# Expert rows scattered by index to (choice, token) order, and a combine that reads plain tiles, in a two-layer mixture-of-experts kernel

## The reference, cut to what matters

```python
expert = g_idx * EXP_PER_GROUP + e_idx          # [n, 2]: two choices for each token, of 32 experts
...
ys = (jax.nn.silu(xb @ w1[e]) * (xb @ w3[e])) @ w2[e]     # for each block of rows of one expert e
...
out[token] = sum over its two choices of gate * ys[row of that choice]
```

## Time and profile before

| | |
|---|---|
| runs | 3020.61, 3024.97, 3027.89 us; median 3024.97 |
| profiled execution | 3028.9 us; span of its trace 3027.1 us |
| PE busy | 88% of the span, mean granted clock 0.935 |
| DVE, ACT, POOL busy | 41%, 22%, 14% |
| DMA | 594.60 MB, mean 196 GB/s |
| experts of layer 0 | about 1606 to 2140 us, 42 blocks |
| experts of layer 1 | about 2534 to 2972 us, 51 blocks |

### The profile page before, as it was taken

One profiled execution on the slowest core, in us unless ns is written; L12 is line 12 of the kernel. 1 busy time (PEld: TensorE's weight loads), 2 busy tenths in 40 slices (PEclk: granted clock), 3 DMA queues, 4 the chain that ended last, 5 costly groups with the idle time before them and its releaser, 6 DMA issues. The chain is left out here.

```text
span 3027.1 us, 44944 instructions
## 1 busy us (share of the span) xinstructions
PE 2662.8 (88%) x17074; PEld 1742.1 (58%) x17075; DVE 1226.9 (41%) x2425; ACT 652.6 (22%) x1342; POOL 414.1 (14%) x465
## 2 busy tenths in 40 slices
PE   7999989999999998989968998889698984898755
PEld 5877766488884574557545554445444642454333
DVE  5752367248999922127162111111513623222114
ACT  3540178120000010117131000000321631010002
POOL 3432012014440000000001100000100001121101
PEclk9999999999999999989988999999899996999877
DMA  3231320137545632120028889999722025999994
GB/s 141 91 126 60 137 78 26 63 100 234 209 182 224 243 139 76 41 78 1 28 76 328 355 353 421 411 413 387 260 86 91 1 88 216 353 386 382 404 420 148
DMA packets 137319, 594.60 MB, mean 196 GB/s; under 512 B 20336, under 2 KB 40588, under 8 KB 90608
## 3 DMA queue, kind: packets, MB, share of 16 engines
q1 hardware_dynamic: 86704, 359.25, 31.5%
q10 hardware_dynamic: 41808, 212.75, 17.6%
q0 software_dynamic: 8688, 21.00, 1.9%
HBM read 574.06 MB, written 33.69 MB: 201 GB/s over the span
## 5 line engine op out<-in xcount | busy, mean ns | idle before, releaser
L1406 DVE SCALAR_TENSOR_TENSOR psum<-weight_ring,condition_rows 128x1024 f32<-128x1024 f32 x192 | 268.1, 1396 | 16.0 <-issue 0.9
L174 PE MATMUL psum<-modulated,weight_ring 128*128 128x384 f32 (+2 forms) x640 | 228.7, 518 | 0.0
L2826 DVE COPY expert_hidden_turned<-psum 128x128 f32<-128x128 f32 (+1 forms) x93 | 32.6, 351 | 462.6 <-PE psum L2684 462.6
L2673 PE MATMUL psum<-weight_ring,slot_rows_turned 128*32 128x256 f32 x2176 | 145.9, 414 | 77.2 <-DMA weight_ring<-in_w_dram 46.1
L2662 PE MATMUL psum<-weight_ring,slot_rows_turned 128*64 128x256 f32 x1792 | 205.6, 383 | 0.6 <-issue 0.6
L174 PEld LDWEIGHTS psum<-modulated,weight_ring 128*128 128x128 f32 x640 | 121.4, 190 | 105.5 <-issue 51.0
L2754 ACT ACTIVATE expert_silu<-psum 64x256 f32<-64x256 f32 (+1 forms) x91 | 34.6, 380 | 659.5 <-PE psum L2662 347.7
L2662 PEld LDWEIGHTS psum<-weight_ring,slot_rows_turned 128*64 128x64 f32 x1792 | 127.5, 138 | 76.3 <-issue 16.9
L2691 PE MATMUL psum<-weight_ring,expert_hidden_turned 128*32 128x256 f32 (+1 forms) x1536 | 165.8, 441 | 0.0
L174 PE MATMUL psum<-ffn_hidden,weight_ring 128*128 128x512 f32 (+1 forms) x440 | 154.5, 514 | 4.1 <-DVE ffn_hidden L1451 4.1
L2812 DVE TENSOR_TENSOR expert_hidden<-expert_silu,psum 64x256 f32<-64x256 f32 (+1 forms) x93 | 39.2, 422 | 276.7 <-ACT expert_silu L2754 248.7
(11 more groups left out here) (476 smaller groups left out, 4332.8 us busy)
## 6 DMA issues: line engine op xcount, KB each, us to landing
third_stream_weights<-in_w_dram ACTq DMA_DIRECT2D x93, 2048.0 KB, 14.6
weight_ring<-in_w_dram SPq DMA_DIRECT2D x84, 2048.0 KB, 17.5
weight_ring<-in_w_ada_dram SPq DMA_DIRECT2D x24, 2048.0 KB, 9.2
weight_ring<-in_w_ffn_dram SPq DMA_DIRECT2D x11, 2048.0 KB, 12.3
weight_ring<-in_w_rnn_dram SPq DMA_DIRECT2D x8, 1536.0 KB, 6.6
weight_ring<-in_w_att_dram SPq DMA_DIRECT2D x6, 2048.0 KB, 8.1
weight_ring<-in_w_in_dram SPq DMA_DIRECT2D x6, 2048.0 KB, 13.5
weight_ring<-in_w_down_dram SPq DMA_DIRECT2D x8, 1408.0 KB, 6.2
```

What stands on the lines that cost most here:

```text
L174: last = nc.tensor.matmul(out, weights[:, k * P:(k + 1) * P], rhs(k), start=(k == 0), stop=(k == tiles - 1))
L1406: last = v.scalar_tensor_tensor(out=product, in0=w[:, t], scalar=1.0, in1=CR[:, n, :], op0=ALU.mult, op1=ALU.mult, accum_out=c.mod[:, i // ...
L2673: last = nc.tensor.matmul(ps[units.rows(2 * m + o), 2 + b, 0:256], XT[:, b, k % tiles, units.rows(k // tiles)], w[:, k, 256 * o:256 * (o + ...
L2826: v.tensor_copy(HT[:, b, :, :], ps[:, 1, 0:256].rearrange("p (k s) -> p k s", k=2)[:, :, 0:2 * cap])\
```

## The change

Each expert block is no longer stored in place by ACT. POOL scatters it with an indirect DMA, 128 partial rows by index, to a DRAM tensor of 2 x 768 rows in (choice, token) order; rows of empty slots have an index past the end and are skipped. `route` computes a second index table for it, `R.home`, from which `R.index` is now derived with two more VectorE instructions, and no longer computes `R.slot`. The combine reads plain tiles of 128 rows, issued by SP. Since every row that is read has been written, the zero fill is gone. Three scatters whose indices are all past the end are issued before the loop, so that the counts of the semaphores begin at 16.

The core of the diff:

```diff
@@ feed_forward
-                written = UNITS[0].least * UNITS[0].cap
-                sp.dma_start(c.expert_out[written:, :], c.ios["zeros"].partition_broadcast(SLOTS - written))\
-                    .then_inc(zeros_in, 16)
                 ring.uses += len(order)
                 ring.feed(sp, ring.uses + Ring.SLOTS)
-                sp.wait_ge(zeros_in, 16)
@@ second_setup
-    c.expert_out = nc.dram_tensor("expert_rows", (SLOTS, D), F32, kind="Internal").ap()
+    c.expert_out = nc.dram_tensor("expert_rows", (2 * T, D), F32, kind="Internal").ap()
@@ route
-                v.scalar_tensor_tensor(out=R.slot[:, :, 0:nt], in0=blk, scalar=float(cap), in1=place,
-                                       op0=ALU.mult, op1=ALU.add)
...
-                v.tensor_scalar(R.index[:, 0:nblk], ps[:, 5, 0:nblk], const("half"), None, ALU.add).then_inc(placed.sem, 1)
+                to, wrapped, own = BL[:, 0, 0, 0:nblk], BL[:, 0, 1, 0:nblk], float(units_of.groups * units_of.tokens)
+                v.tensor_scalar(to, ps[:, 5, 0:nblk], const("half"), None, ALU.add)
+                dve.drain()
+                v.tensor_scalar(wrapped, to, own, -own, ALU.is_ge, ALU.mult)
+                dve.drain()
+                v.tensor_tensor(R.index[:, 0:nblk], to, wrapped, ALU.add).then_inc(placed.sem, 1)
+                v.tensor_copy(R.home[:, 0:nblk], to)
@@ experts, POOL
-                with pool.Fori(0, rounds(pool)) as it:
+                def store_at(b):
+                    pool.indirect_dma_start(out_rows, bass.IndirectOffsetOnAxis(HOME[:, b:b + 1], 0), YS[:, b, :], None,
+                                            bounds_check=2 * groups * units.tokens - 1, oob_is_err=False)\
+                        .then_inc(y_out[b].sem, 16)
+
+                def home(n, b, copied):
+                    if copied is None:
+                        last_copied.wait(pool, b + 1)
+                    else:
+                        y_copied.wait(pool, copied)
+                    nc.gpsimd.tensor_copy(HOME[:, b:b + 1], R.home[:, bass.ds(n, 1)])
+                    pool.drain()
+                    store_at(b)
+
+                for b in range(NSTREAM):
+                    nc.gpsimd.tensor_copy(HOME[:, b:b + 1], R.home[:, units.most - 1:units.most])
+                nc.gpsimd.memset(YS[:, :, :], 0.0)
+                pool.drain()
+                for b in range(NSTREAM):
+                    store_at(b)
+                last = rounds(pool)
+                with pool.Fori(0, last) as it:
                     for b in range(NSTREAM):
                         x_turned.wait(pool, it * NSTREAM + b + 1)
                         nc.gpsimd.tensor_copy(IDX[:, b:b + 1], R.index[:, bass.ds(it * NSTREAM + b + NSTREAM, 1)])
...
                             .then_inc(gathered[b].sem, 16)
+                        home(it * NSTREAM + b, b, it * NSTREAM + b + 1)
+                for b in range(NSTREAM):
+                    home(last * NSTREAM + b, b, None)
@@ experts, ACT
                 def store(n, b, it):
-                    y_out[b].wait(act, it * (16 * groups))
+                    y_out[b].wait(act, it * 16 + 16)
                     nc.scalar.copy(YS[:, b, :], ps[:, 5 + b, 0:cols]).then_inc(y_copied.sem, 1)
-                    y_copied.wait(act, n + 1)
-                    for o in range(groups):
-                        act.dma_start(out_rows[bass.ds(n, 1)].rearrange("b s d -> s (b d)")[:, units.part(o)],
-                                      YS[units.rows(o), b, :]).then_inc(y_out[b].sem, 16)
@@ combine_and_norm
-            @block.gpsimd
-            def _(pool):
-                for i in range(nt):
-                    if i >= NBUF:
-                        turned.wait(pool, i - NBUF + 1)
-                    for k, y in enumerate((Y1[i % NBUF], Y2[i % NBUF])):
-                        pool.indirect_dma_start(y, None, c.expert_out,
-                                                bass.IndirectOffsetOnAxis(R.slot[:, k, i:i + 1], 0))\
-                            .then_inc(rows_in[i % NBUF].sem, 16)
@@ combine_and_norm, SP
+                for i in range(nt):
+                    if i >= NBUF:
+                        turned.wait(sp, i - NBUF + 1)
+                    for k, y in enumerate((Y1[i % NBUF], Y2[i % NBUF])):
+                        at = (k * nt + i) * P
+                        sp.dma_start(y, c.expert_out[at:at + P, :]).then_inc(rows_in[i % NBUF].sem, 16)
```

More of the change, by code:

```diff
@@ L1549, in _ @@
                 ring.feed(sp, ring.uses + Ring.SLOTS)
-                sp.wait_ge(c.x_in, 32)
+                sp.wait_ge(c.x_in, 16)
         p_in.passed(16)
@@ L1586 @@
 NSTEP = max(u.steps for u in UNITS)
-SLOTS = max(u.most * u.cap for u in UNITS)
 NKEY = 2 * NEXP
@@ L2238, in __init__ @@
         self.LGT = ctx.enter_context(c.nc.sbuf_tensor(f"logits_turned_{l}", [RW, T], F32))
-        self.IDS, self.ROW = sb("token_ids", [P, TT]), sb("token_row", [P, 3, D])
+        self.IDS, self.ROW = sb("token_ids", [P, 2 * TT]), sb("token_row", [P, 3, D])
         self.consts = c.sig("route_consts_landed")
@@ L2497, in _ @@
                     dve.drain()
-                    v.tensor_tensor(BL[:, k, 0:nt, :], BL[:, k, 0:nt, :], n3(IDS[:, 0:nt], nblk), ALU.mult)\
+                    v.tensor_tensor(BL[:, k, 0:nt, :], BL[:, k, 0:nt, :], n3(IDS[:, k * TT:k * TT + nt], nblk), ALU.mult)\
                         .then_inc(placed.sem, 1)
-                v.scalar_tensor_tensor(out=R.slot[:, :, 0:nt], in0=blk, scalar=float(cap), in1=place,
-                                       op0=ALU.mult, op1=ALU.add)
                 number, movable, keys = const("number"), const("movable"), KEYS[:, 0, :]
@@ L2566, in sb @@
             return ctx.enter_context(c.nc.sbuf_tensor(f"{name}_{l}", shape, dt))
-        self.slot, self.gate = sb("slots", [P, 2, TT], U32), sb("expert_gates", [P, 2, TT], F32)
+        self.gate = sb("expert_gates", [P, 2, TT], F32)
+        self.home = sb("slot_home", [P, UNITS[l].most], U32)
         self.index, self.plan = sb("slot_index", [P, UNITS[l].most], U32), sb("expert_plan", [1, NTABLE * UNITS[l].most], U32)
@@ L2585, in sb @@
             return ctx.enter_context(nc.sbuf_tensor(f"{name}_{l}", shape, dt))
-        IDX = sb("gather_index", [P, NSTREAM], U32)
+        IDX, HOME = sb("gather_index", [P, NSTREAM], U32), sb("home_index", [P, NSTREAM], U32)
         XT = sb("slot_rows_turned", [P, NSTREAM, tiles, P])
@@ L2592, in experts @@
         sm = lambda n: Signal(c.sem(f"moe{l}_{n}"))
-        again = lambda n: c.spare.pop(0) if len(c.spare) > 5 - 5 * l else sm(n)
+        again = lambda n: c.spare.pop(0) if len(c.spare) > 3 - 3 * l else sm(n)
         XS, part_rows, gathered = R.rows, R.part_rows, R.gathered
-        y_out = [sm("y_stored0"), c.spare.pop(), c.spare.pop()]
+        y_out = [sm(f"y_stored{b}") for b in range(NSTREAM)]
         landed = [sm(f"weights_landed{m}") for m in range(3)]
@@ L2603, in experts @@
         third_copied = c.sig("third_stream_copied")
-        primed = [(s, PRIMED) for s in counted] + [(s, 1) for s in y_out + [third_copied]] + [(s, 16) for s in landed]
+        primed = [(s, PRIMED) for s in counted] + [(s, 1) for s in [third_copied]] + [(s, 16) for s in landed]
         for s, n in primed:
@@ L2608, in experts @@
         slot0 = [ring.slot(first_chunk + m) for m in range(3)]
+        last_copied = c.sig("combine_turned")
         all_stored, all_landed = c.sig("moe_all_stored"), c.sig("moe_all_landed")
-        out_rows = c.expert_out.rearrange("(b s) d -> b s d", s=cap)
+        out_rows = c.expert_out.rearrange("t (h n) -> (t h) n", h=groups)
         entry = lambda table, n: R.plan[0:1, bass.ds(n + table * units.most, 1)]
@@ L2799, in _ @@
                     store(n, b, last)
+                    act.drain()
+                    act.sem_inc(last_copied.sem, 1)
                 for b in range(NSTREAM):
-                    y_out[b].wait(act, last * (16 * groups) + 16 * groups)
+                    y_out[b].wait(act, last * 16 + 32)
                 act.sem_inc(all_stored.sem, 1)
@@ L2881, in experts @@
             s.passed(1)
+        last_copied.passed(NSTREAM)
         for n in range(Ring.SLOTS):
@@ L3155, in second_arrays @@
         "causal_bias": arrays["slopes"][0][:, None, None] * arrays["causal_dist"][None],
-        "ctxT": g("ctx")[0].T, "zeros": np_.zeros((1, D), np_.float32),
+        "ctxT": g("ctx")[0].T,
         "cond": g("c"), "cond_ctx": g("c_ctx")[None, :],
@@ L3170, in second_arrays @@
         "router_consts": consts,
-        "token_ids": np_.stack([u.groups * (np_.arange(TT)[None, :] * P + np_.arange(P)[:, None]) - NOWHERE
+        "token_ids": np_.stack([np_.concatenate([u.groups * (np_.arange(TT)[None, :] * P + np_.arange(P)[:, None]
+                                                             + k * u.tokens) - NOWHERE for k in range(2)], 1)
                                 for u in UNITS]).astype(np_.float32),
```

1 line of the change is left out of this document (removed).

## The result

The changed kernel takes 3232.39 us in the median of 4 runs (3225.23 to 3234.59), the kernel before 3024.09 beside it (3020.61 to 3027.89): a ratio of 1.0684, with a 95% interval of 1.0663 to 1.0706. That is 208 us slower. The forecast was 3270 us, so the sign and the mechanism held and the size was 38 us too large.

What follows compares the result with a forecast made beforehand. Layer 0 was held limited by PE and weights, layer 1 mostly by weights; afterwards POOL's two serial drained transfers. 3028.9 + 250 - 1 = 3278, less 3.9 for the median: 3274, forecast 3270 us; range 3180 to 3360, wider 3090 to 3430.

Steps and rivals of the forecast that it cites:

- The drain waits for POOL's earlier transfer: Expert loop: `pool.drain()` ahead of a transfer waits until POOL's earlier indirect one lands; 8.7 or 7.6 us slow, 4.1 or 4.0 fast.
- The scatter behaves like the gather of the same block: Expert loop: no scatter in the trace before, so its landing was taken as equal to the same block's gather.
- rival B: Only layer 1 suffers, a little: short scatter, slow gather, +85 us, layer 0 unchanged; 3110 us, or 3055; chance 0.14.
- The term of +250 us: Expert loops of both layers: two drained transfers in series per block on POOL; middle of 212 and 289 us.
- The tiling rule: Expert loops: B weight time, s slow, f fast transfer; period B + f(2 - B/s), 13.9 and 11.5 us; costs 212 us.
- chance: Expert loops: each transfer meets busy engines with chance B/period; period 2f + 2(s - f)B/period, 14.8 and 12.3 us; costs 289 us.
- The zero fill: 0: Feed-forward part: dropping the 46.3 us fill gains 0, since the product hides it; without that cover, 20 us.
- Stores off ACT, and fewer bytes: 0: Expert loops: four fewer ACT issues worth 0; fewer bytes, 11 and 6 us of DMA time, worth 0 with POOL the limit.
- The combine: 2 us less in each layer, the end of the experts 1 us more: Plain first loads save 2 us per layer; POOL's copy, drain and scatter at the experts' end add about 1 us.
- What would show it: Profile after: POOL issues 4 to 8 us apart without waiting for PE or ACT; periods 14 to 15 and 11.5 to 12.5 us.
- Rival A: Expert loops: the scatters fit into the block, so not slower, and fewer bytes count; about 3010 us; chance 0.11.
- rival C: Expert loops: no relief, transfers meet full DMA engines nearly always; +350 to +540, 3375 to 3565 us; chance 0.13.

Runs made afterwards that it cites:

- lighter weights: Changed kernel with the third stream's second and third weight loads in the loop cut from 2048 to 512 KB each: 3125.28 us; same cut before the change: 2934.10 us.

## Why the prediction was right, and where its size was off

- **The drain waits for POOL's earlier transfer.** Right, and shown twice: by the 85 steps that take the scatter's landing plus 0.87 us, and by the run without drains, which gives 191 of 207 us back with the same transfers.
- **The scatter behaves like the gather of the same block.** Nearly. In layer 0 it lands in 6.6 us (median; gathers there 6.8). In layer 1 it lands in 3.3 (gathers 6.1): there 25 of 50 scatters went out while the weight queues paused, against 12 of 47 gathers. That the pauses come from PE's waiting is how I read it, without a run for it. So rival B named something real, and still fell: both layers suffer, since layer 1's two transfers together stay far above 8.36 us.
- **The term of +250 us was mis-sized.** It was the middle of two estimates, 212 (slow transfers tile the time in which weights move) and 289 (each meets them by chance). The runs show 210 us: 1.70 x 41 + 2.80 x 50. The tiling rule gave 57 + 155, so it is right in the sum and 13 to 15 us off in each layer, in opposite directions. Had I taken it by itself, the forecast would have been 3236 us. But its nearness does not show that tiling is right. The landings in the two loops can be counted: call a transfer slow when it lands in more than 4 us. The rules' shares of slow transfers are B/period (chance) and B/2s (tiling).

| kernel, layer | slow (chance, tiling) | period measured | chance, measured prices | tiling, measured prices |
|---|---|---|---|---|
| after, 0 | 72% (75, 61) | 14.18 | 14.1 | 13.3 |
| after, 1 | 61% (65, 48) | 11.16 | 11.7 | 10.8 |
| lighter weights, 0 | 63% (63, 47) | 12.93 | 12.7 | 11.9 |
| lighter weights, 1 | 47% (48, 32) | 9.97 | 10.3 | 9.4 |

  The shares stand with chance. The size that was wrong is the price: with the 0.87 us behind the landing, a slow transfer of the changed kernel cost 8.1 us in layer 0 and 7.2 in layer 1, not 8.7 and 7.6, and a fast one 3.9 and 3.5, not 4.1 and 4.0. The measured prices put three of the four periods nearer to chance. With the line at 5 us instead of 4, both periods of layer 1 come out nearer to tiling, so between the rules it stays open there. That tiling hit the sum with prices that are too high is in part luck.
- **POOL full.** Both rules count POOL's own time alone. In layer 1's loop that holds: two mean landings and twice 0.87 us make 11.5 us, and the loop takes 11.4 for a block. In layer 0 they make 13.8 and the loop takes 14.6: the rest is the wait for ACT's copy, which neither rule has.
- **The zero fill: 0.** Right within the 5 us that the run with the fill put back can tell.
- **Stores off ACT, and fewer bytes: 0.** ACT's queue carries 17.7 MB less (212.75 to 195.04 MB) and POOL's scatters write 10.5 MB (its queue's 21.02 MB less the 10.57 with empty scatters), so 7.2 MB are saved, with nothing gained. The page's line of HBM writes is no measure of it: it counts skipped rows too, since it shows 26.21 MB here and 32.51 MB, the same plus its 6.29 MB of fill, in the kernel whose scatters write nothing. With the drains gone, layer 1 came out 0.12 us a block below before (6 us), which may be these bytes or the four issues; it wasn't taken apart.
- **The combine: 2 us less in each layer, the end of the experts 1 us more.** Roughly right. The timeline of the kernel after in layer 1, against the earlier trace rows:

```profile
3178.60 0.37 ACT L2784 COPY expert_rows<-psum 128x256 f32<-128x256 f32 x1 [2.55 <-PE psum L2714]
3180.62 0.99 POOL L2623 DMA_INDIRECT expert_rows<-expert_rows,home_index  x1 [1.26 <-issue]
3183.33 4.59 SPq L3060 DMA_DIRECT2D choice_rows<-expert_rows  x8
3188.34 1.15 ACT L3031 ACTIVATE choice_rows<-choice_rows,expert_gates 128x1024 f32<-128x1024 f32 x1 [9.36 <-DMA choice_rows<-expert_rows]
```

  From first load to first scaling 5.01 us instead of 6.46, and from the last copy to the first load 4.73 instead of 4.48: 1.2 us less in all, and 1.5 in layer 0 (11.34 to 9.86). I had counted 1.
- **What would show it.** PE's waits, the falling DMA share and the lower clock came as described; the shares were 0.82 and 0.72, not 0.75 and 0.65. One line was wrong: POOL does wait for ACT's output copy, 92.3 us in layer 0. A fast scatter leaves it time. The other sign of being wrong, scatters under 3 us beside full engines, did not come: the fastest there took 3.9 us in layer 1 and 4.4 in layer 0. The period of layer 1 (11.16) was just under the 11.5 to 12.5 I gave.
- **The rule of the pages.** By the 2.0 us plus bytes over 436 GB/s of the Trainium skill ("DMA: Bandwidth & Descriptors", section "Anatomy of one DMA — SWDGE (gpsimd) path") the change would have been free. The measurement decides against it here: only the fastest transfers (2.1 to 2.8 us) come near it, and beside full engines the medians are 6 to 9 us.

Rival A fell with the result (1.068), rival C too: relief came, and more of it than I had assumed.

## What to carry to other kernels

A drain on POOL ahead of an indirect transfer waits for the landing of the one before. One such transfer in a period can be free while the second costs a full landing, so let another engine write the index and order POOL by a semaphore. Price such a queue by landing time beside the real traffic, not by bytes, and look for the ring: if what lands late holds back the engine whose result releases the next issue, the loss is larger than the queue's own sum. Where an estimate lies between two rules, a sum that matches one of them does not settle it: count in the trace how often each case occurs and what each costs.

## What the runs showed of the hardware that I had not expected

POOL pays for indirect transfers that it has not drained. In the kernel with the scatter a block later the drain at the end of layer 1's experts, the first after 101 transfers, takes 9.6 us in the trace and ends 7.4 us after their last packet; in layer 0, after 83 transfers, it takes 8.1 us and ends 5.7 after. With an early drain the last one covers 4 transfers and takes 2.7 and 3.0 us, ending 0.5 us after the last packet. By these four drains the difference is 0.065 to 0.07 us for each transfer. The two early drains themselves took 11.0 and 10.2 us, beside PE's work on the last blocks. Removed drains are not wholly free: part of their work is put off to the next one, which should stand where POOL has time.
